# Root sums from high and low squares, and another order of attention steps and groups, in a two-block transformer kernel

## The reference

```python
def rms_norm(x, g):
    xf = x.astype(jnp.float32)
    y = xf * lax.rsqrt(jnp.mean(xf * xf, axis=-1, keepdims=True) + EPS)
    return (y * g.astype(jnp.float32)).astype(x.dtype)
...
    qf = rms_norm_2(q, gq).astype(jnp.float32) * (dh ** -0.5)
    kf = rms_norm_2(k, gk).astype(jnp.float32)
```

## Time and profile before

| | |
|---|---|
| median of three runs | 3640.29 us (3638.33 to 3644.27) |
| the profiled execution | 3637.62 us, span 3635.8 us |
| PE busy | 3447.4 us, 95% |
| GpSimd busy | 2373.3 us, 65% |
| VectorE busy | 1442.9 us, 40% |
| ScalarE busy | 777.5 us, 21% |
| mean granted TensorE clock | 0.983 |

### The profile page before, as it was taken

The page is one execution under the profiler, slowest core; times in us unless marked ns, Lnnn a source line. Parts: engine busy times, 40 slices in busy tenths (PEclk is TensorE's granted clock), DMA queues, the critical chain, the costliest instruction groups (busy, mean ns, idle before and its releaser), DMA issues.

```text
span 3635.8 us, 42471 instructions
## 1 busy us (share of the span) xinstructions
PE 3447.4 (95%) x17034; PEld 2746.0 (76%) x17034; DVE 1442.9 (40%) x2757; ACT 777.5 (21%) x1572; POOL 2373.3 (65%) x1238
## 2 busy tenths in 40 slices
PE   7876999999999999988999999999999889999999
PEld 6553666888898888656778888888887557788887
DVE  5765654343353235564433111332345644332111
ACT  2544332111121002243212100110012432211000
POOL 6413444887768776633668777787776435678775
PEclk9988999999999999989999999999999999999999
DMA  3212122354435442211232222254432112232222
GB/s 137 65 58 70 57 65 68 108 197 168 167 117 210 175 176 99 82 53 55 85 96 102 99 99 95 91 203 164 166 128 76 53 56 82 79 105 98 93 99 76
DMA packets 104196, 388.09 MB, mean 107 GB/s; under 512 B 11824, under 2 KB 12080, under 8 KB 97856
## 3 DMA queue, kind: packets, MB, share of 16 engines
q1 hardware_dynamic: 87984, 292.76, 23.6%
q10 hardware_dynamic: 16016, 92.62, 6.7%
HBM read 383.20 MB, written 2.13 MB: 106 GB/s over the span
## 4 chain that ended last, share of the span: by engine, by line
PE 86%; DVE 8%; ACT 3%; issue 2%; DMA 0%; ACTq 0%; DVEq 0%
PE psum L1138 27%; PE psum L1139 26%; PE psum L1140 26%; PE psum L1211 2%; PE psum L1253 2%; PE psum L1228 2%; DVE rs_t L1544 2%; DVE s_sb L1584 1%; PE psum L1197 1%; ACT s_sb L1366 1%; DVE neg_max L1589 1%; DVE s_sb L1621 1%; ACT sq_t L1340 0%; DMA small<-first_small_dram 0%; ACT L1348 0%
## 5 line engine op out<-in xcount | busy, mean ns | idle before, releaser
L1106 POOL TENSOR_TENSOR w_hi<-raw,ones 128x1024 fp32r<-128x1024 f32 (+3 forms) x591 | 1042.6, 1764 | 1090.8 <-PE psum L1140 1081.7
L1109 POOL TENSOR_TENSOR w_lo<-raw,w_hi 128x1024 fp32r<-128x1024 f32 (+3 forms) x591 | 1316.0, 2227 | 46.5
L1138 PE MATMUL psum<-h_hi,w_hi 128*128 128x512 f32 (+2 forms) x2912 | 1148.5, 394 | 42.7 <-DVE r L1559 29.9
L1139 PE MATMUL psum<-h_lo,w_hi 128*128 128x512 f32 (+2 forms) x2912 | 1108.9, 381 | 0.0
L1140 PE MATMUL psum<-h_hi,w_lo 128*128 128x512 f32 (+2 forms) x2912 | 1108.7, 381 | 0.0
L1138 PEld LDWEIGHTS psum<-h_hi,w_hi 128*128 128x128 f32 (+1 forms) x2912 | 552.5, 190 | 191.0 <-issue 41.9
L1140 PEld LDWEIGHTS psum<-h_hi,w_lo 128*128 128x128 f32 (+1 forms) x2912 | 552.1, 190 | 107.6
L1139 PEld LDWEIGHTS psum<-h_lo,w_hi 128*128 128x128 f32 (+1 forms) x2912 | 553.5, 190 | 99.4 <-issue 6.3
L1138 PE MATMUL psum<-a_hi,w_hi 128*128 128x512 f32 (+1 forms) x1064 | 392.5, 369 | 0.0
L1139 PE MATMUL psum<-a_lo,w_hi 128*128 128x512 f32 (+1 forms) x1064 | 391.8, 368 | 0.0
L1140 PE MATMUL psum<-a_hi,w_lo 128*128 128x512 f32 (+1 forms) x1064 | 391.8, 368 | 0.0
(11 more groups left out here) (189 smaller groups left out, 3400.0 us busy)
## 6 DMA issues: line engine op xcount, KB each, us to landing
raw<-weights_dram SPq DMA_DIRECT2D x489, 512.0 KB, 3.3
ada_t<-ada_dram ACTq DMA_DIRECT2D x48, 1536.0 KB, 7.1
raw<-weights_dram SPq DMA_DIRECT2D x72, 256.0 KB, 2.6
raw<-weights_dram SPq DMA_DIRECT2D x32, 384.0 KB, 3.0
bias_t<-biases_dram ACTq DMA_DIRECT2D x36, 256.0 KB, 2.8
bias_t<-cum_dram ACTq DMA_DIRECT2D x16, 256.0 KB, 3.7
out_dram<-x SPq DMA_DIRECT2D x8, 256.0 KB, 2.0
raw<-weights_dram SPq DMA_DIRECT2D x4, 408.0 KB, 3.0
```

What stands on the lines that cost most here:

```text
L1106: nc.gpsimd.tensor_tensor(high, piece, ones[:, 0:1].to_broadcast([P, n]), ALU.mult)\
L1109: nc.gpsimd.tensor_tensor(w_lo[:, p % NR, 0:n], piece, high.bitcast(F32), ALU.subtract)\
L1138: mm(dst, lh, rh, start=first, stop=False)
L1139: mm(dst, lh, rl, start=False, stop=False)
```

## The change

There are three edits.

The root sum. sq_t keeps for each root a high part and a low part in fp32r instead of two fp32 squares in turn. ScalarE squares the source twice, into sq_t[0], rounded to fp32r, and into the sum bank in fp32. VectorE subtracts the two into sq_t[1]. PE multiplies both by fp32r ones, in two products that add up in the sum bank. The squares are put at once when LATER is empty, and go into LATER as a fourth entry when it is not. As a root's PE step can now be put later than a group that needs its bank, mm() empties LATER up to that root. A differential output is first copied by ScalarE (`ocopy`), and its squares read the copy. The ones are tiles of their own that GpSimd writes.

The attention's beats. In att_b, att_c and att_c2 scores and values become one beat with twice the weight, turn and copy one, and scale the third. In att_a and att_a2 the four beats stay.

The order beside att_a2. The groups were f, u and then q, k, v; now q, k, u and v are mixed and two pairs of q and k stand at and near the end.

```diff
@@ mm()
+        while g.before and g.before[0] == "qk_out" and g.before[1] > ROOTED[0]:
+            LATER.pop(0)[1]()
@@ new_root()
-    put("qsq", q)
-    def total():
+    def squares():
         q.sum_before = take(SUM_BANK)
         HELD[SUM_BANK] = ("qk_rooted", q.n)
+        put("qsq", q)
+    def total():
         put("qsum", q)
...
         put("qfin", q)
+        ROOTED[0] = q.n
...
+    if LATER:
+        late(squares)
+    else:
+        squares()
     late(total)
@@ attend()
-        if 0 <= j + 1 < n:
-            put("copy", duos[j + 1])
...
+                put("ocopy", u)
                 new_root("differential", ("small", "subln", 0), ("r0", u.pair), u)
...
+    def copy(j):
+        if 0 <= j + 1 < n:
+            put("copy", duos[j + 1])
...
-        out += [(lambda j=j: scores(j), w), (lambda j=j: turns(j), w), (lambda j=j: products(j), w),
-                (lambda j=j: scale(j), w)]
+        if kind in ("att_b", "att_c", "att_c2"):
+            out += [(lambda j=j: (scores(j), products(j)), 2 * w), (lambda j=j: (turns(j), copy(j)), w),
+                    (lambda j=j: scale(j), w)]
+        else:
+            out += [(lambda j=j: scores(j), w), (lambda j=j: turns(j), w), (lambda j=j: (products(j), copy(j)), w),
+                    (lambda j=j: scale(j), w)]
@@ layer()
-    jobs = [f, u[0], forget, u[1], *steps[0][0], u[2], steps[0][1], *steps[1][0], u[3], steps[1][1]]
-    chain = [s for ss, prod in steps[2:] for s in ss + [prod]]
-    rest = [q[0], k[0], q[1], k[1], q[2], k[2], q[3], k[3]] + token_groups((l, "vc"), S, "v1", ring)
-    for i, g in enumerate(rest):
-        jobs.append(g)
-        jobs += chain[2 * i:2 * i + 2] if i < 11 else chain[2 * i:]
+    groups = [q[0], u[0], k[0], u[1], q[1], u[2], k[1], u[3], q[2], k[2], *token_groups((l, "vc"), S, "v1", ring),
+              q[3], k[3]]
+    jobs, chain = [f], []
+    for g in groups:
+        jobs += [g] + chain[:2]
+        chain = chain[2:]
+        if g is u[0]:
+            jobs.append(forget)
+        if g in u:
+            shifts, product = steps[u.index(g)]
+            chain += shifts + [product]
+    jobs += chain
@@ GpSimd
+            nc.gpsimd.memset(pair_ones[:], 0.0).then_inc(sem["pool_chain"], 1)
...
+                nc.gpsimd.memset(pair_ones[rows, rows], 1.0).then_inc(sem["pool_chain"], 1)
@@ PE, root_sum()
-                E.wait_ge("qk_squared", q.n)
-                E.wait_at(q.sum_before)
-                lhs = ones[:] if q.what == "differential" else pair_ones
-                mm(bank(SUM_BANK), lhs, sq_t[:, q.n % 2, :], start=True, stop=True).then_inc(sem["qk_summed"], 1)
+                E.wait_ge("qk_low", q.n)
+                lhs = ones_r if q.what == "differential" else pair_r
+                mm(bank(SUM_BANK), lhs[:], sq_t[:, 0, :], start=True, stop=False)
+                mm(bank(SUM_BANK), lhs[:], sq_t[:, 1, :], start=False, stop=True).then_inc(sem["qk_summed"], 1)
@@ ScalarE, root_square()
-                if q.n > 2:
-                    E.wait_ge("qk_summed", q.n - 2)
+                if q.n > 1:
+                    E.wait_ge("qk_summed", q.n - 1)
...
-                fn(sq_t[:, q.n % 2, :], src, ACT.Square).then_inc(sem["qk_squared"], 1)
+                fn(sq_t[:, 0, :], src, ACT.Square).then_inc(sem["qk_squared"], 1)
+                E.wait_at(q.sum_before)
+                fn(bank(SUM_BANK), src, ACT.Square).then_inc(sem["qk_squares"], 1)
@@ VectorE
+                elif what == "qsq":
+                    q = step[1]
+                    E.wait_ge("qk_squared", q.n)
+                    E.wait_ge("qk_squares", q.n)
+                    v.tensor_tensor(sq_t[:, 1, :], bank(SUM_BANK), sq_t[:, 0, :].bitcast(F32), ALU.subtract)\
+                        .then_inc(sem["qk_low"], 1)
```

More of the change, by code:

```diff
@@ L40 @@
 LY_N = 617
-CS = dict(ident=0, pair_ones=128, tri=256, window=384, chunk=512, cmask=640, valid=764, inv_count=765)
-CS_N = 765 + 64
+CS = dict(ident=0, tri=128, window=256, chunk=384, cmask=512, valid=636, inv_count=637)
+CS_N = 637 + 64
 ROOTS = dict(model=(1 / D, EPS), query=(1.0, HALF * EPS), key=(1 / HALF, EPS),
@@ L69 @@
 H_USED = [0]
+ROOTED = [0]
 ADA_AT = [0]
@@ L217, in new_root @@
     q = Root(what, gain, dest, src, tick("qk_squared"))
-    for name in ("qk_summed", "qk_rooted", "qk_out"):
+    for name in ("qk_squares", "qk_low", "qk_summed", "qk_rooted", "qk_out"):
         assert tick(name) == q.n
     tick("qk_inverse", PARTS)
-    put("qsq", q)
-    def total():
+    def squares():
         q.sum_before = take(SUM_BANK)
         HELD[SUM_BANK] = ("qk_rooted", q.n)
+        put("qsq", q)
+    def total():
         put("qsum", q)
@@ L944, in build @@
         cst = sb("cst", [P, CS_N])
-        ones = sb("ones", [P, P])
+        ones_r = sb("ones", [P, P], F32R)
+        pair_r = sb("pair_ones", [P, P], F32R)
+        ones, pair_ones = ones_r[:].bitcast(F32), pair_r[:].bitcast(F32)
         mod_raw = sb("mod_raw", [P, 2, MODS])
@@ L980, in build @@
         merged = at("merged", 58, [P, KC, S])
-        sq_t = at("sq_t", 66, [P, 2, S])
+        sq_t = at("sq_t", 66, [P, 2, S], F32R)
         rs_t = at("rs_t", 70, [P, 2, S])
@@ L1060, in build @@
         ident = cst[:, CS["ident"]:CS["ident"] + P]
-        pair_ones = cst[:, CS["pair_ones"]:CS["pair_ones"] + P]
         names = SEMS + [f"loaded{i}" for i in range(NR)] + ["act_chain", "dve_chain", "pool_chain", "out_done"]
@@ L1086, in _ @@
             E.settle()
+            nc.gpsimd.memset(pair_ones[:], 0.0).then_inc(sem["pool_chain"], 1)
+            E.settle()
+            for half in TWO:
+                rows = slice(half * HALF, (half + 1) * HALF)
+                nc.gpsimd.memset(pair_ones[rows, rows], 1.0).then_inc(sem["pool_chain"], 1)
+                E.settle()
             nc.gpsimd.memset(zeros[:], 0.0).then_inc(sem["pool_chain"], 1)
@@ L1331, in root_square @@
             def root_square(q):
-                if q.n > 2:
-                    E.wait_ge("qk_summed", q.n - 2)
+                if q.n > 1:
+                    E.wait_ge("qk_summed", q.n - 1)
                 if q.what == "differential":
-                    E.wait_ge("pv", q.src.n)
-                    src = bank(O_BANK)
+                    E.wait_ge("oa_copied", q.dest[1] + 1)
+                    src = region["r0"][:, q.dest[1], :]
                 else:
@@ L1339, in root_square @@
                     src = bank(q.src.bank)
-                fn(sq_t[:, q.n % 2, :], src, ACT.Square).then_inc(sem["qk_squared"], 1)
-                if q.what == "differential":
-                    fn(region["r0"][:, q.dest[1], :], src, ACT.Copy).then_inc(sem["oa_copied"], 1)
+                fn(sq_t[:, 0, :], src, ACT.Square).then_inc(sem["qk_squared"], 1)
+                E.wait_at(q.sum_before)
+                fn(bank(SUM_BANK), src, ACT.Square).then_inc(sem["qk_squares"], 1)
             def root(q):
@@ L1435, in _ @@
                     root_square(step[1])
+                elif what == "ocopy":
+                    u = step[1]
+                    E.wait_ge("pv", u.n)
+                    fn(region["r0"][:, u.pair, :], bank(O_BANK), ACT.Copy).then_inc(sem["oa_copied"], 1)
                 elif what == "qsum":
@@ L1959 @@
     consts = np.concatenate([
-        i == j, i // HALF == j // HALF, np.where(j > i, NEG, 0), np.where(j <= i, NEG, 0),
+        i == j, np.where(j > i, NEG, 0), np.where(j <= i, NEG, 0),
         np.where((i < HALF) & (j >= HALF), NEG, 0),
```

## The result

| | before | after |
|---|---|---|
| median of four runs | 3640.23 us (3638.33 to 3644.27) | 3702.91 us (3699.14 to 3704.53) |
| the profiled execution's span | 3635.8 us | 3702.2 us |
| mean granted TensorE clock | 0.983 | 0.969 |

The ratio is 1.0169, 95% interval 1.0152 to 1.0187: slower by 63 us, where 3650 was forecast and 3676 was the upper end of the range. The sign was right and most of the places were; the size was not.

The account below looks back on a forecast made before the run. PE was taken to bound the kernel, 86% of the chain that ended last. The terms -23 + 37 + 28 + 5 - 26 - 10 gave +11 us, forecast as 3650 us, range 3617 to 3676.

Parts of the forecast that it names:

- Shorter sums, -23: Root sums on PE: two fp32r products instead of one fp32 save 0.41 us, 55 times, -23 us.
- Attention order, -26: att_b, att_c and both att_c2: fewer fp32 changes and shorter turn waits, -26 us.
- att_c2 near 168: Sign to look for in the profile: each att_c2 stage takes near 168 us.
- The order in att_a2, -10: Both att_a2: one forced bank wait replaces two, and a pool product waits; -5 us each, -10 together.
- The forced bank: att_a2: query 2, pool product 2 and key 2 share a bank; a wait of 7.1 us and 2 of slow products.
- The q and k stretches, +28: A layer's q and k, twice: the queue never drains, bank waits and clock loss cost +14 us each, +28.
- I take about one such loss more per stretch: q and k stretches: one more loss of clock behind a wait, about 1.7 us, in each.
- the 70 to 76 of the sign: Sign to look for: a layer's q and k stretch takes 70 to 76 us instead of 60.4.
- clearly slower: Rival, chance 0.14: every repeated wait in q and k and att_a2 halves the clock, VectorE's queue adds more; 3677 us.
- The chain ahead of a sum, +37: Roots in att_a, att_b and att_a2: second square and subtraction delay 23 sums by 1.4 us; with differential roots +37.
- they start 0.6 to 0.7 late, inside the 1.4: ScalarE's and VectorE's next steps queue behind the new root work; their delay was counted within the chain's 1.4 us.
- first q and k +5: The kernel's first q and k: a longer period of the queue, +5 us without the sums' saving.

Follow-up runs that it names:

- attend_only: The kernel before with only the new beats of att_b, att_c and att_c2: 3617.09 us, ratio 0.993.
- order_only: The kernel before with the new attention beats and the new order beside att_a2, root sums still fp32: 3598.96 us, ratio 0.988.
- high_only: The changed kernel without second square, subtraction and second product, the sum made of the squares' high part alone: 3626.81 us, ratio 0.9961.
- busy_both_b: The changed kernel with unread products put in q and k bank waits and ahead of att_a2 sums that directly follow their squares: 3678.27 us, ratio 1.0096.
- order_only_b: The same program as order_only, run again for comparison: 3604.21 us, ratio 0.9885 to the kernel before.

## Why the prediction was wrong

**Shorter sums, -23.** Right where it can be read. The two records of a sum start 0.23 apart (1507.85, 1508.08) at 0.39 and 0.40 us; in the loop before, the second product starts 0.69 us behind the sum's start (1497.83 to 1498.52), against 1.10 in the earlier trace rows: 0.41 saved.

**Attention order, -26.** attend_only: -25, of it -7.5 in att_b and -11.4 in att_c, with -8 and -13 forecast. What failed in it is att_c2: fewer changes between fp32 and fp32r should have given 3.5 us each, and they gave 1.1. The sign "att_c2 near 168" does not follow from the sum either: 174.7 less 3.5 and 1 more is 172.2, and 175.2 was measured. In att_c the size came out nearly right by another way than forecast. All 13 us were to come from PE's idle time and nothing from fewer changes; by the rows of after and the earlier trace rows PE idles 15.1 us instead of 21.3, and the other 5.3 come out of its busy time (229.5 instead of 234.9). The turns gave back half of their waits there, 13.9 to 7.1. Values waited 7.0 us for their copies in all of after.

**The order in att_a2, -10.** order_only against attend_only: -14, in the stages -11.1 and -10.4, and att_c2 +1.6 each where +1 was forecast. Together the orders are 3.4 us better than forecast. The forced bank was priced well (one wait of 6.5 us for 7.1), but two things that the term left out took each other nearly away: in each att_a2 the new order raised the waits ahead of sums from 11.1 to 17.1 us, and the turns' waits fell from 7.5 to 0.8. The pool product, put at 2.5, did not wait in order_only.

**The q and k stretches, +28; "I take about one such loss more per stretch".** This step failed, though everything else in it held: the waits were forecast as 1.7, 5.1 and four of 2.4 and came as 1.46, 4.96, 2.25, 2.24, 2.25, 2.24. The clock loss came behind each of the last five in the first layer, not once: some five times 1.7 us instead of one. The stretch ended 18.2 later with the sums' saving in it, forecast 11.2, and at 78.6 us lies above the 70 to 76 of the sign, in the step that was trusted most. The rival "clearly slower" had this mechanism and was given 0.14; the argument against it, that waits of 0.69 have no loss behind them, says nothing about waits of 2.2, and the one of that size that the prediction had read did have it.

**The chain ahead of a sum, +37.** This is the term that missed most. The waits in it were sized well: the sums that follow their squares wait 1.97 instead of 0.69. But the term priced only these waits, as if nothing followed from them ("they start 0.6 to 0.7 late, inside the 1.4"). Without the sums' saving the root change cost some 26 us in att_a and 49 in the two att_a2 (21.3 and 42.8, plus 0.41 for each of their 11 and 16 sums), where the term had 9 and 22.

high_only tells how much of it is the chain. Without the second product's 0.23 us per sum, the second square and the subtraction cost 22.2 and 23.4 us in the two att_a2, 11.8 in att_a and 2.4 in att_b: 60 us, where the term had 37. In the first att_a2 the waits ahead of sums are 10.2 of it, a pool product pushed under GpSimd's work 4.7, and the clock at least 5.3 (busy_both_b). These two, the instructions under GpSimd and the clock, are what followed from the waits and was put at nothing.

The other 18 us stand in high_only too, without the chain, 14 of them in att_a. There the waits ahead of sums rose from 7.5 to 17.0 us, 9.5 more, as forecast. The scores waited 23.1 us for VectorE (all of the L1246 line above) instead of 17.2, but that is not the chain's doing, since they wait 25.4 in high_only. The clock fell from 0.96 to 0.89 and PE's busy time rose from 112.9 to 118.9 us; this isn't shown to come from the root change at all: no kernel filled the waits in att_a, and order_only_b had 0.89 and 144.8 us without it, the time of high_only. The four kernels with the full chain and the same queue were at 157.3 to 159.0.

**The sum.** With forecast and measured side by side, the sums' saving taken out of each and shown alone: sums -23 and -23; chain +37 and +78 (26 in att_a, 49 in att_a2, 3 in att_b); q and k +28 and +42.5; first q and k +5 and +8; orders -36 and -39. That is +11 forecast and +66 measured. Of the error of 55 us the chain's term holds 41, of which high_only bears out 23, and the clock behind repeated waits of q and k 14.5. With order_only_b as the base the root change costs 7 us less, all of it in att_a.

What stays open: some 2 us of the first att_a2 (24.0 less 10.2, 4.7, 5.3 and the second products' 1.8), which may be clock that the fillers did not save, and the 14 us of att_a beyond the chain, which the fourth entry of the queue, the new `ocopy` and the clock's variation between executions share in a way that no run parts.

## What to carry to other kernels

Price a wait of TensorE by its length and by the slow products that may stand behind it: in after's loop 2.25 us of idle cost 3.96, four times in a row, while the same wait cost only itself elsewhere. So a loop of such waits is a range with both prices as its ends, and not one number. Where an in-order engine gets a longer chain ahead of a step, count also who is queued behind it on the other engines, and which of them it pushes under GpSimd's. A later step trades one wait for another, here for a bank held longer or for later probabilities; try it stage by stage, and take orders and arithmetic apart: here two good edits hid under a third that cost 2.7 times their gain.

## What the runs showed that was not expected

- A wait of 2.25 us is followed by some 3.4 us at the lower clock even when 7.6 us of unbroken work stood before it, four times in a row. The same program had the full clock behind a like wait of 2.22 us in one layer and 0.63 in the other (attend_only).
- Unread products in such waits made the kernel faster: 13 us in all for some 50 products per q and k stretch.
- A copy of two columns on VectorE took 2.24 us instead of 0.17 under GpSimd's splitting; the same holds for two more instructions, and PE waited 4.9 us for them.
- The same program's att_a differed by 7 us between two executions at equal idle time of PE, with the granted clock at 0.95 and 0.89. That is a third of the loss that the root change seemed to cost there.
